# The mixer's stick-breaking attention with keys on partitions, and its attention steps laid between products

## The reference

```python
h = rms_norm(x, mix_norm)
q_n, kc, vc, ks, vs, kw, vw, gates, q_s, k_s, v_s = split(h @ w_in)      # 2840 columns
o_nsa = nsa_mixer(...)     # 8 heads: compressed, selected and window attention, each a softmax, summed by gates
o_sb = stick_breaking(q_s, k_s, v_s)                                     # 8 heads of 64
x = x + concatenate([o_nsa, o_sb], axis=-1) @ w_out

def stick_breaking(q, k, v):              # per tile of 128 queries
    z = einsum('bhqd,bhkd->bhqk', q, k) * dk ** -0.5
    mask = kpos < tq                      # strictly before the query
    log_rem = where(mask, log_sigmoid(-z), 0.0)
    suffix = cumsum(log_rem, reverse=True) - log_rem
    a = where(mask, exp(log_sigmoid(z) + suffix), 0.0)
    return einsum('bhqk,bhkd->bhqd', a, v)
```

## Time and profile before

| | us |
|---|---|
| median of three runs | 1338.25 (1333.71 to 1339.14) |
| profiled execution, its own time | 1333.12 |
| its span | 1331.2 |
| PE busy | 1266.3 (95%) |
| DVE busy | 732.6 (55%) |
| ACT busy | 543.3 (41%) |
| POOL busy | 78.2 (6%) |
| mean granted clock of PE | 0.946 |

### The profile page before, as it was taken

The page is one execution under the profiler, slowest core; times in us unless marked ns, Lnnn a source line. Parts: engine busy times, 40 slices in busy tenths (PEclk is TensorE's granted clock), DMA queues, the critical chain, the costliest instruction groups (busy, mean ns, idle before and its releaser), DMA issues.

```text
span 1331.2 us, 14684 instructions
## 1 busy us (share of the span) xinstructions
PE 1266.3 (95%) x6107; PEld 1053.9 (79%) x6107; DVE 732.6 (55%) x743; ACT 543.3 (41%) x645; POOL 78.2 (6%) x123
## 2 busy tenths in 40 slices
PE   6998999999999899999989999999999887899998
PEld 5886888888889778888868888888877775788887
DVE  4657455554556655655356555467868645455552
ACT  4533344443455344544245444344425232444441
POOL 4100000000100010100010000021110000000000
PEclk9998999999999999999999999999865595899999
DMA  7753466556583246655546555465503012275550
GB/s 268 253 190 127 140 209 189 183 181 221 187 258 126 94 129 217 212 164 216 187 142 190 190 190 210 138 205 170 190 1 103 24 64 79 70 244 181 184 207 32
DMA packets 145777, 218.45 MB, mean 164 GB/s; under 512 B 5136, under 2 KB 111664, under 8 KB 145584
## 3 DMA queue, kind: packets, MB, share of 16 engines
q1 hardware_dynamic: 142592, 206.69, 46.8%
q0 software_dynamic: 3120, 10.84, 2.3%
HBM read 216.45 MB, written 1.05 MB: 163 GB/s over the span
## 4 chain that ended last, share of the span: by engine, by line
PE 87%; DVE 7%; ACT 2%; issue 2%; POOL 1%; DMA 1%; SPq 0%; DVEq 0%; POOLq 0%; ACTq 0%
PE acc L1495 26%; PE acc L1497 25%; PE acc L1496 25%; PE turn L1481 3%; PE acc L1621 2%; PE turn L1637 2%; DVE w_lo L943 1%; PE turn L1646 1%; DVE xt L953 1%; DMA raw<-in_a_w_in 1%; ACT w_hi L691 1%; PE acc L1730 1%; PE turn L1710 0%; DMA posi<-in_positions_ends_t 0%; DVE xn L968 0%
## 5 line engine op out<-in xcount | busy, mean ns | idle before, releaser
L943 DVE TENSOR_TENSOR w_lo<-raw,w_hi 128x2048 fp32r<-128x2048 f32 x196 | 442.2, 2279 | 198.3 <-ACT w_hi L691 198.1
L1495 PE MATMUL acc<-w_hi,xt 128*128 128x512 f32 (+2 forms) x1144 | 450.7, 394 | 17.6 <-DVE xt L953 15.0
L1497 PE MATMUL acc<-w_hi,xt 128*128 128x512 f32 (+2 forms) x1144 | 443.9, 388 | 0.0
L1496 PE MATMUL acc<-w_lo,xt 128*128 128x512 f32 (+2 forms) x1144 | 443.2, 387 | 0.0
L691 ACT ACTIVATE w_hi<-raw 128x2048 fp32r<-128x2048 f32 x196 | 367.5, 1907 | 139.4 <-PE acc L1497 109.0
L1495 PEld LDWEIGHTS acc<-w_hi,xt 128*128 128x128 f32 x1144 | 218.6, 191 | 62.8 <-DVE xt L953 16.0
L1497 PEld LDWEIGHTS acc<-w_hi,xt 128*128 128x128 f32 x1144 | 218.1, 191 | 44.1
L1496 PEld LDWEIGHTS acc<-w_lo,xt 128*128 128x128 f32 x1144 | 218.8, 191 | 41.4
L1495 PE MATMUL acc<-w_hi,ht 128*128 128x512 f32 x352 | 139.6, 397 | 0.0
L1497 PE MATMUL acc<-w_hi,ht 128*128 128x512 f32 x352 | 138.0, 392 | 0.0
L1496 PE MATMUL acc<-w_lo,ht 128*128 128x512 f32 x352 | 136.6, 388 | 0.0
(11 more groups left out here) (238 smaller groups left out, 977.7 us busy)
## 6 DMA issues: line engine op xcount, KB each, us to landing
raw<-in_ffn_w_gate_up SPq DMA_DIRECT2D x88, 512.0 KB, 5.0
raw<-in_ffn_w_down SPq DMA_DIRECT2D x22, 1024.0 KB, 5.0
raw<-in_ffn_wg SPq DMA_DIRECT2D x44, 512.0 KB, 4.1
raw<-in_ffn_wu SPq DMA_DIRECT2D x44, 512.0 KB, 5.1
raw<-in_ffn_wd SPq DMA_DIRECT2D x22, 1024.0 KB, 5.1
raw<-in_a_w_in SPq DMA_DIRECT2D x16, 1024.0 KB, 6.0
raw<-in_w_in SPq DMA_DIRECT2D x10, 1024.0 KB, 5.3
raw<-in_a_w_out SPq DMA_DIRECT2D x8, 1024.0 KB, 5.1
```

Source lines behind the costliest of these rows:

```text
L943: V.tensor_tensor(w_lo[:, u % RING, 0:kt * w], raw[:, u % RAW, 0:kt * w], w_hi[:, u % RING, 0:kt * w].bitcast(F32), ALU.subtract).then_inc ...
L1495: mm(o, lhs[0], rhs[0], start=start, stop=False)
L1496: mm(o, lhs[0], rhs[1], start=False, stop=False)
L1497: return mm(o, lhs[1], rhs[0], start=False, stop=stop)
```

## The change

- *Stick-breaking* has keys on partitions. PE makes the scores of a head as [keys, queries], adds a large negative number where the key isn't before the query (a product of the identity with `unseen`), ACT takes the softplus; PE makes the same scores again and adds to them the products of a lower triangle (`upto`) and of a full block (`after`, for the second tile of keys) with the softplus, so that the bank holds the logarithm of the share; ACT takes the exp; the shares stand as the values' product needs them, with no turning. The output comes out with features on partitions, so ACT and DVE split it straight into `xt`. Scans, sigmoids, POOL's mask and the turned shares are gone.
- *Stick queries and keys* come from products with the weights stationary (`sqk_tile`), already turned; `z` no longer holds them. The units of `w_in_2` stand in another order, and those of `w_out_2` begin with the stick rows.
- *Order.* Stick steps stand between the products of queries, keys, values and the compressed branch; the selected and window steps (six, of both halves at once, `STEPS2`) stand between tiles of memory and output products. The output product is made tile by tile and half by half (`mixed_tile`): first the stick rows, later the rows of the other heads.
- *Banks* may be emptied by ACT as well (`freed`); a wait for a bank is then on `s_afree`.

The core of the diff: new functions, and the new orders on the three engines.

```diff
+    U_MIN = len(units)
+    for c0, n in ((BLK, BLK), (0, BLK), (2 * BLK, Z_SQ - 2 * BLK)):
...
+    U_SQK = [len(units)]
+    for c0 in (Z_SQ, Z_SK):
+        units.append((KD, 256, [(0, part(ins["w_in_2"], 0, KD, c0, 256))]))
...
+    for k0 in (4, 6, 0, 2):
+        units.append((2, D, [(0, part(ins["w_out_2"], k0 * P, 2, 0, D))]))
...
+            def stick_logs(b):
+                if b:
+                    act.wait_ge(s_sbpv, b)
+                for h in range(4):
+                    n = N_SB[b] + h
+                    act.wait_ge(s_turned, n + 1)
+                    nc.scalar.activation(stick[:, h, :], tb[n % 4][:, 0:384], ACT.Softplus, scale=SCALE).then_inc(s_sp, 1)
+            def stick_weights(b):
+                for h in range(4):
+                    act.wait_ge(s_tri, 4 * b + h + 1)
+                    nc.scalar.activation(stick[:, h, :], tb[(N_SB[b] + h) % 4][:, 0:384], ACT.Exp,
+                                         scale=SCALE).then_inc(s_afree, 1)
...
+            split_to(U_MIN + 14)
+            stick_logs(0)
+            read_sqk(1, 0)
+            split_to(U_MIN + 15)
+            stick_weights(0)
+            read_sqk(1, 1)
+            split_to(U_MIN + 16)
+            stick_high(0)
+            stick_logs(1)
+            split_to(U_MIN + 18)
+            stick_weights(1)
+            act.wait_ge(s_used, U_CMP + 4)
+            nc.scalar.activation(hidg[:], acc[0][0:32, :].rearrange("p (i m) -> p i m", i=2),
...
+            stick_high(1)
+            split_to(U_MOUT + 2)
+            exps2(0)
+            split_to(U_MOUT + 3)
+            exps2(1)
+            act.wait_ge(s_used, U_MKV + 2)
...
+            exps2(2)
+            split_to(U_MOUT + 4)
...
+            split_to(U_MOUT + 1)
+            shift2(0)
+            turned_hidden()
+            split_to(U_MOUT + 2)
+            shares2(0)
+            shift2(1)
+            compressed_heads()
+            shares2(1)
+            split_to(U_MOUT + 3)
+            shift2(2)
+            compressed_keys()
+            part_out(0, 0)
+            part_out(1, 0)
+            shares2(2)
+            compressed_scores()
+            shift2(3)
+            split_to(U_MOUT + 4)
+            compressed_shares()
+            shares2(3)
+            shift2(4)
+            compressed_out()
+            sum_out(0)
+            shares2(4)
+            shift2(5)
+            norm_heads(1)
+            low_on(0)
+            part_out(0, 1)
+            shares2(5)
+            copy_bank(N_MKT, mqt[:, 2:4, :].rearrange("p k n -> p (k n)"))
+            part_out(1, 1)
+            sum_out(1)
+            residual(5, C_MO, U_MOUT + 3, 0)
+            scaled(X, R_MEMX, G_MEMX, 0)
+            low_on(1)
...
+            def stick_group(j, two, stop):
+                diagonal = spread(unseen_r[:], [[0, 2], [1, P]])
+                for c0, n, k0 in ((0, TOK, 0), (TOK, P, P)):
+                    for half in range(2):
+                        rows = slice(HEAD * half, HEAD * half + HEAD)
+                        mm(two[half][:, c0:c0 + n], skt[rows, j, k0:k0 + P], sqt[rows, j, TOK - n:TOK],
+                           start=k0 == 0, stop=False)
+                return [mm(bank[:].rearrange("p (a n) -> p a n", a=2)[:, :, 0:P], ident_r[:], diagonal, start=False, stop=stop)
+                        for bank in two]
...
+                    mm(two[half][:, 0:384], upto[:], stick[:, h, :], start=False, stop=False)
+                    mm(two[half][:, P:TOK], after[:], stick[:, h, TOK:384], start=False, stop=True).then_inc(s_tri, 1)
...
+            def mixed_tile(t, half, nsa):
+                for i in range(2 * nsa, 2 * nsa + 2):
+                    u = U_MOUT + i
+                    pe.wait_ge(s_lo, u + 1)
+                    for k in range(2):
+                        at = (4 + 2 * i + k) % KD
+                        last = product(acc[2 * ((C_MO + half) % 2) + t][:], [xt[0][:, hl, at, t * P:(t + 1) * P] for hl in range(2)],
...
+            by_columns_block(U_MB, C_MIN + 2, xt_hl(0))
+            pe.wait_ge(s_read, C_MIN + 2)
+            sqk_tile(0, 0, 0)
+            compressed_inputs()
+            sqk_tile(0, 0, 1)
...
+            by_columns_block(U_SV, C_MIN + 3, xt_hl(0))
+            pe.wait_ge(s_kq, 10)
+            stick_scores(0)
+            pe.wait_ge(s_read, C_MIN + 4)
+            sqk_tile(1, 0, 0)
+            stick_sums(0, 0)
+            sqk_tile(1, 0, 1)
+            stick_sums(0, 1)
+            for e in range(2):
+                sqk_tile(1, 1, e)
+            stick_values(0)
...
+            compressed_unit(0)
+            compressed_unit(1)
+            for j in range(2):
+                stick_sums(1, j)
+            compressed_unit(2)
+            compressed_unit(3)
+            stick_values(1)
+            scores2(0)
+            memory_product(0, 0)
+            pe.wait_ge(s_chid, 1)
+            turned_hidden()
+            turn_shares2(0)
+            scores2(1)
+            memory_product(0, 1)
+            pe.wait_ge(s_sbo, 2)
+            values2(0)
+            compressed_heads()
+            turn_shares2(1)
+            scores2(2)
+            memory_product(1, 0)
+            values2(1)
+            compressed_keys()
+            memory_product(1, 1)
+            turn_shares2(2)
+            compressed_scores()
+            scores2(3)
+            pe.wait_ge(s_read, C_MKV + 1)
+            mixed_tile(0, 0, 0)
+            values2(2)
+            compressed_shares()
+            turn_shares2(3)
+            scores2(4)
+            mixed_tile(0, 1, 0)
+            values2(3)
+            compressed_out()
+            turn_shares2(4)
+            scores2(5)
+            turn_on(0)
+            values2(4)
+            pe.wait_ge(*freed(T_ON[0][0]))
+            mixed_tile(0, 0, 1)
+            turn_shares2(5)
+            mixed_tile(0, 1, 1).then_inc(s_half, 1)
+            values2(5)
...
+            mixed_tile(1, 0, 0)
+            pe.wait_ge(s_swr, 4)
+            mixed_tile(1, 1, 0)
+            turn_on(1)
+            pe.wait_ge(*freed(T_ON[1][0]))
+            mixed_tile(1, 0, 1)
+            turn_rows(T_MX, G_MEMX, 0)
+            mixed_tile(1, 1, 1)
```

More of the change, by code:

```diff
@@ L191, in banks_list, with freed @@
         return list(range(banks(n), n_at[0]))
+    def freed(n):
+        before = len([x for x in ACT_FREED if x < n])
+        return (s_afree, before + 1) if n in ACT_FREED else (s_tfree, n + 1 - before)
     T_NORM_A = splits(4)
@@ L908, in _, with read_sqk @@
[L908 to L913 removed]
+            def read_sqk(b, i):
+                act.wait_ge(s_used, U_SQK[b] + i + 1)
+                dst = (sqt, skt)[i][:, 2 * b:2 * b + 2, :].rearrange("p k n -> p (k n)")
+                nc.scalar.activation(dst, acc[2 * i][:], ACT.Copy).then_inc(s_kq, 1)
@@ new lines, in stick_high, with exps2 @@
+            def stick_high(b):
+                act.wait_ge(s_used, U_SQK[1] + 2)
+                act.wait_ge(s_sbpv, b + 1)
+                nc.scalar.activation(pair(xt_hl(0), 0, 4 + 2 * b), acc[(3, 1)[b]][:], ACT.Copy).then_inc(s_sbhi, 1)
+            def exps2(i):
+                t, w, js = STEPS2[i]
+                nk = keys_of(t)
+                for g in range(2):
+                    act.wait_ge(s_max, K_SW + 2 * i + g + 1)
+                    for e, j in enumerate(js):
+                        seg = sc2[:, i % 2, g, e * nk:(e + 1) * nk]
+                        last = nc.scalar.activation(seg, seg, ACT.Exp, bias=nm2[:, 2 * i + g, e:e + 1],
+                                                    accum_out=sum2[:, w, t, 4 * g + j:4 * g + j + 1])
+                    last.then_inc(s_exp, 1)
@@ new lines, in _ @@
+            split_to(U_MIN + 6)
+            act.wait_ge(s_built, 3)
+            nc.scalar.activation(ident_r[:], ident[:], ACT.Copy).then_inc(s_masks, 1)
+            nc.scalar.activation(unseen_r[:], unseen[:], ACT.Copy).then_inc(s_masks, 1)
+            read_z(C_MIN, U_MIN + 1, BLK, BLK)
+            split_to(U_MIN + 7)
+            read_z(C_MIN + 1, U_MIN + 3, 0, BLK)
+            act.wait_ge(s_ang, 1)
+            for i in range(2):
+                nc.scalar.activation(trig[:, i, :, 0, :], angr[:, i], ACT.Sin).then_inc(s_trig, 1)
@@ L1822, in _ @@
-            pe.wait_ge(s_clo, 1)
-            b = take(N_CHID)
-            for i in range(2):
-                for l in range(16):
-                    u = U_CMP + 2 * i + l // 8
-                    if l % 8 == 0:
-                        pe.wait_ge(s_lo, u + 1)
-                    last = product(b[0:32, i * CMP_HID:(i + 1) * CMP_HID], [x[:, i, l, :] for x in cmp_hl],
-                                   weights(u, l % 8, CMP_HID), l == 0, l == 15)
-                    if l % 8 == 7 and (i, l) != (1, 15):
-                        last.then_inc(s_used, 1)
@@ new lines, in compressed_inputs @@
+            def compressed_inputs():
+                bank = take(N_CSEL)
+                for i in range(2):
+                    for g in range(2):
```

(25 more changed lines are left out.)

514 lines of the change are left out of this document (269 added, 245 removed).

## The result

The changed kernel takes 1314.88 us (median of four runs, 1314.78 to 1315.5). Beside it the kernel before took 1338.32 us (four runs, 1333.71 to 1339.14); the ratio is 0.983, with a 95% interval of 0.981 to 0.986: faster, by 1.7%, clear of 1. Forecast was 1322, range 1304 to 1342. The two profiled executions lie closer together than the medians, 1333.12 and 1314.8 us, 18.3 apart. Over all series of this study the kernel before ran 38 times, 1329.8 to 1339.1, median 1335.1; against that the change is worth 20 us, and that is the size to keep in mind.

What follows compares the result with a forecast made beforehand. The granted clock, not waits, was taken to bound the mixer stage. PE work 166.3, norm 7.7, waits 24.0, handovers 3 and clock 6 made 207 us against 223.2, 16 less: 1322 us from the median, range 1304 to 1342.

Steps and rivals of the forecast that it cites:

- What bounds the kernel: Mixer stage of 223.2 us: in its 110.3 us of attention the clock, 0.61, sets the time, PE being busy 101.2.
- The first part: Stage start to stick values: 96 us of PE work at full clock, about 1.3 us idle, done about 967 us.
- One reading of the rows: Selected and window item shapes, in the first block's attention between products, run at clock 1.00 and cost half.
- The stick terms: PE's new stick-breaking work: scores 8.7, triangle products 7.4, values 5.6, sum 21.7 us; softplus on ACT taken as 0.5.
- The waits: PE waits, mostly after the stick values: sum 24.0 us, the longest 6.6 for the first tile's heads; handovers 3 more.
- The clock of the second part: Stick values to output product: clock 0.855, midway between 0.71 and 1.00, costing 11 us, about half hidden in waits, so 6.
- The end: Whole kernel: 16 us less gives 1317 from the profiled execution, 1322 from the median of 1338.25; 1322 forecast.
- why the clock stays up: Attention steps: the change puts products between nearly all of them, where small products alone had let the clock fall.
- A: Rival: clock stays up in the second part and waits shrink by up to half; 1316, at best 1304; chance 0.27.
- B: Rival: after the stick values small stretches run, and products start, at half clock; stage 226, kernel 1341; chance 0.16.
- C: Rival: products between steps too short to restore the clock, second part all at half clock; 1362; chance 0.07.
- D: Rival: the steps' chains, above all DVE's, are longer, with twice the waits, 24 us more; 1346; chance 0.07.

Runs made afterwards that it cites:

- 10: Changed kernel with DVE's and ACT's lists reordered and memory products moved so that each stands in a wait, no work added: 1290.4 us, 0.967 of the kernel before.
- 1: Changed kernel, on PE alone memory products put ahead of the six selected and window steps and the output product behind them: 1322.5 us, 7.6 slower.
- 11: Kernel before with 72 unread products of 512 columns added ahead of the shares of six of twelve selected and window items: 1337.2 us, ratio 1.001.
- 9: Changed kernel with no product between attention steps, stick steps and selected and window steps both bare: 1321.1 us, 0.990 of the kernel before.
- 2: Changed kernel with bare stick steps: second pair of stick query and key products ahead of them, compressed units behind: 1319.5 us, 4.6 slower.
- 12: Changed kernel with bare stick steps, plus ACT making the first softplus ten times more so that PE waits: 1325.6 us, 6.1 more than without the wait.
- 5: Changed kernel, DVE's list: memory keys' norm halved, first half ahead of the compressed output, second behind the first tile's heads' split: 1308.6 us, 6.3 faster.
- 6: Changed kernel with step 0 of selected and window attention ahead of the output weights' splits on DVE and ACT: 1313.0 us, 1.9 faster.

## Why the prediction was right, step by step

- *What bounds the kernel: the clock, not a wait.* Right, and more than it said: work is equal, idle time grew, and 27 us of lost clock are gone.
- *The first part, done at about 967 us at full clock.* Measured 966.9, clock 1.00, 98.0 us of work and no idle time where 96 and 1.3 were forecast.
- *One reading of the rows.* The shapes of an item were said to cost half at full clock. For values and transposes show that; of scores, eight instructions take 1.13 us between products and four took 2.07, about a quarter. The price in the sum, 1.13, was the right one.
- *The stick terms.* PE and ACT of the changed kernel in time order (start, duration, operation, count):

```profile
921.92 0.92 PE L1948 MATMUL turn<-sqt,skt 64*128 64x256 f32 x8
922.78 0.50 PE L1950 MATMUL turn<-unseen_r,ident_r 128*128 128x256 f32 x2
923.21 0.92 PE L1948 MATMUL turn<-sqt,skt 64*128 64x256 f32 x8
...
927.37 0.92 PE L1948 MATMUL turn<-sqt,skt 64*128 64x256 f32 x8
928.22 0.50 PE L1950 MATMUL turn<-unseen_r,ident_r 128*128 128x256 f32 x2
928.56 0.81 PE L1967 MATMUL turn<-stick,upto 128*128 128x384 f32 x2
929.21 0.38 PE L1968 MATMUL turn<-stick,after 128*128 128x128 f32 x2
929.42 0.81 PE L1967 MATMUL turn<-stick,upto 128*128 128x384 f32 x2
```

```profile
942.03 0.66 PE L1977 MATMUL acc<-stick,z 128*64 128x256 f32 x4
...
943.54 1.53 PE L1593 MATMUL turn<-ident,work 128*128 128x128 f32 x12
```

```profile
926.23 1.64 ACT L913 ACTIVATE stick<-turn 128x384 f32<-128x384 f32 x4
```

  Scores with their mask take 923.21 - 921.92 = 1.29 us a pair the first time and 928.56 - 927.37 = 1.19 the second (1.1 forecast). The triangle, 929.42 - 928.56 = 0.86 a head (0.93). Values of four heads 943.54 - 942.03 = 1.5 us, so 3.0 in all instead of 5.6: that term was mis-sized by nearly two. Softplus 1.64 / 4 = 0.41 (0.5). In all 4 x 1.29 + 4 x 1.19 + 8 x 0.86 + 3.0 = 19.8 us against 21.7.
- *The waits.* Step 0 3.57 us (3.7), the second halves of steps 0 and 1 and step 1's w_hi 2.5 (2.7), the heads of the first tile 6.3 (6.6), of the second 2.7 (2.6), the exps of step 2 2.27 (2.8), values of step 4 0.8 (0.7; it stands ahead of the turned heads just before them). Too much was the compressed keys (0.5 for 1.9) and the compressed shares, where PE did not wait (1.7). With the 3 us of handovers, which do not show as waits, 27 us were forecast, 25.7 of them in the second part, which is idle for 19.3.
- *The clock of the second part.* 0.86 measured, 0.855 taken as the middle of two rows. That it meets is luck: no row gave this value for these steps, and by 10 the same steps in another order run at 0.96. The low clock cost 10.5 us, 11 were forecast, and half of that was to lie in waits. If that is why the idle time is 6.4 less than forecast, or if waits were priced too high, the runs don't separate. Idle time and lost clock together are 29.8 us, 31.7 by the forecast; with the stick terms, 1.9 less, most of the difference between 207 and the 202.7 measured is told.
- *The end.* From the profiled execution 1317 was forecast and 1314.8 measured. The forecast of 1322 was put on the median of three runs, which lies 3 us above that of all 38.
- *Where it was wrong: why the clock stays up.* The forecast gave it to products between the steps. That is so for the selected and window steps (1 and 11), but undoing it costs 6 to 8 us of the 20 (1, 9). A second part lies in the new stick steps: they hold full clock with no product near them (2, 9) and bring it back after a wait (12), where the old stretch of 951 to 998.5 us stood at 0.71. The third part has no cause shown: bare selected and window steps lose 16.8 us from 977 to 1043 in 9, where those of the kernel before lost 26.7 from 1003.4 to 1061.3, although the compressed branch comes on top in 9.
- *The rivals.* A (clock stays up) is refuted at 0.86, but 10 shows what it is worth: 0.96, and 1290. B and C (each step starts at half clock, and products are too short to bring it back) fall with the 0.86, and with 11, where 2.7 us of products between items held 1.00. D (longer chains) falls with 19.3 us of idle time. The Trainium skill, "TensorE: Matmul & The Clock Gate", section "HAM oscillation", tells that work after a long gap starts at the low level. The traces agree at each long wait (0.50 behind those of 3.6 to 6.3 us), and 12 shows the way back as well. But the clock also fell without a wait (at 994.2 in 10, at 975.3 in the kernel before).

Left open: why the selected and window steps alone (1) bring the clock back so seldom although PE is busy there, and why they lose less with the stick steps bare as well (9: 16.8 us from 977 to 1043, against 21.5 in the same steps of 1). What the shape of a matmul counts for was not measured by itself. The steps that held the clock and those that did not differ in several things at once: transposes, matmuls of 16 and 64 columns, scores that alternate between the two halves of the rows. No run changes one of these alone.

## What to carry to other kernels

Split a stage's time into work at full clock, clock loss and idle time before pricing a change: here two kernels with the same work on TensorE differ by 20 us. Where attention items with transposes and matmuls of 64 to 256 columns followed one another at 0.5, dense products between them were nearly free (16.4 us of them cost 2). And after such a change go for the waits that are left: taking 4.5 us of waiting away gave 6.3 us in 5, though 2.6 us gave only 1.9 in 6. Moving instructions in three lists, on top of the change, was worth 24.5 us, more than the 20 of the change itself.

## What was not expected of the hardware

- The clock follows more than how long PE is busy: 31.3 of 31.6 us busy at 0.50 (kernel before, 1003.4 to 1035), 22.0 of 22.9 at 1.00 (2).
- Values products into the two halves of the partitions cost half of what their columns suggested, 1.5 us for four heads.
- The kernel before repeats within 9 us (1329.8 to 1339.1), the changed one within 0.7 us and 10 within 0.8. In the runs of the kernel before the mean granted clock lies between 0.941 and 0.950, and the fastest, 1329.8 us, has 0.950.
